# First border of a two-layer diffusion block: TensorE sums the squares tile by tile, and one low part moves ahead in the last head

## What is computed

```python
def readout(o, g):                       # HGRN2, o: heads side by side
    o = o * lax.rsqrt(jnp.mean(o * o, axis=-1, keepdims=True) + EPS)
    o = (o * norm_w.astype(jnp.float32).reshape(HG_HEADS, HG_VDIM)).reshape(b, L, D_MODEL)
    return (o * jax.nn.silu(g.astype(jnp.float32))).astype(g.dtype) @ w_out
...
x = x + mx[2] * rmsnorm(yx, post_norm[l, 0])          # and ctx likewise
hx = modulate(rmsnorm(x, pre_norm[l, 1]), mx[3], mx[4])
yx = conv_ffn(hx, ...)
```

## Time and profile before

| | us |
|---|---|
| median of 3 runs | 1404.38 |
| lowest and highest of them | 1404.37, 1404.94 |
| the profiled execution, its own time | 1403.67 |
| the profiled execution, its span | 1401.9 |
| TensorE busy in the span | 1330.2 |
| VectorE busy | 901.2 |
| ScalarE busy | 646.8 |

### The profile page before, as it was taken

The page is one execution under the profiler, slowest core; times in us unless marked ns, Lnnn a source line. Parts: engine busy times, 40 slices in busy tenths (PEclk is TensorE's granted clock), DMA queues, the critical chain, the costliest instruction groups (busy, mean ns, idle before and its releaser), DMA issues.

```text
span 1401.9 us, 21260 instructions
## 1 busy us (share of the span) xinstructions
PE 1330.2 (95%) x7893; PEld 1118.4 (80%) x7893; DVE 901.2 (64%) x1730; ACT 646.8 (46%) x1020; POOL 305.0 (22%) x203
## 2 busy tenths in 40 slices
PE   5999999999998999999999988999999988899997
PEld 3678888887765888888888756888888877899997
DVE  5567767667587744413446787777777857765573
ACT  4435444444256433223333365455555644554554
POOL 1000000000200653115541000211111300580961
PEclk9999999999999999999999999999999999999999
DMA  9543343334460632334315324433333465365743
GB/s 347 175 136 121 123 134 121 121 116 155 151 212 28 184 101 60 90 106 119 103 54 154 102 92 119 149 92 91 91 91 94 133 203 158 113 172 166 208 135 107
DMA packets 274787, 183.16 MB, mean 131 GB/s; under 512 B 6642, under 2 KB 249106, under 8 KB 274706
## 3 DMA queue, kind: packets, MB, share of 16 engines
q1 hardware_dynamic: 274162, 180.00, 42.6%
q10 hardware_dynamic: 544, 2.10, 0.4%
HBM read 181.03 MB, written 1.05 MB: 130 GB/s over the span
## 4 chain that ended last, share of the span: by engine, by line
PE 77%; DVE 13%; ACT 6%; issue 2%; DMA 1%; SPq 1%; POOL 0%; DVEq 0%; ACTq 0%
PE bank L2092 20%; PE bank L2094 20%; PE bank L2093 20%; DVE wl L1312 3%; ACT tmp L845 1%; DMA gates<-in_ada_w 1%; PE bank L2158 1%; ACT wh L799 1%; DVE hl L1408 1%; DVE tmp L1430 1%; PE bank L2207 1%; DVE conv L1760 1%; PE bank L2234 1%; PE bank L2654 1%; ACT hh L849 1%
## 5 line engine op out<-in xcount | busy, mean ns | idle before, releaser
L2092 PE MATMUL bank<-hh,wh 128*128 128x512 f32 (+1 forms) x1305 | 464.2, 356 | 11.2 <-DVE wl L1312 5.5
L2094 PE MATMUL bank<-hh,wl 128*128 128x512 f32 (+1 forms) x1305 | 459.4, 352 | 0.0
L2093 PE MATMUL bank<-hl,wh 128*128 128x512 f32 (+1 forms) x1305 | 459.1, 352 | 0.0
L799 ACT ACTIVATE wh<-wraw 128x1024 fp32r<-128x1024 f32 (+2 forms) x265 | 256.5, 985 | 100.7 <-PE bank L2094 97.4
L2092 PEld LDWEIGHTS bank<-hh,wh 128*128 128x128 f32 x1305 | 249.1, 191 | 46.4 <-DVE wl L1312 7.8
L1312 DVE TENSOR_TENSOR wl<-wraw,wh 128x1024 fp32r<-128x1024 f32 (+2 forms) x187 | 206.0, 1123 | 122.4 <-ACT wh L799 122.3
L2094 PEld LDWEIGHTS bank<-hh,wl 128*128 128x128 f32 x1305 | 248.8, 191 | 32.9
L2093 PEld LDWEIGHTS bank<-hl,wh 128*128 128x128 f32 x1305 | 249.1, 191 | 30.7
L1760 DVE SCALAR_TENSOR_TENSOR conv<-bank,pv,conv 128x189 f32<-128x189 f32 (+3 forms) x396 | 173.1, 437 | 131.8 <-ACT conv L1064 103.6
L700 POOL TENSOR_TENSOR wl<-wraw,wh 128x1024 fp32r<-128x1024 f32 x78 | 186.8, 2404 | 317.3 <-ACT wh L799 316.6
L2092 PE MATMUL bank<-fh,wh 128*128 128x512 f32 (+1 forms) x352 | 120.1, 341 | 3.4 <-DVE wl L1312 3.1
(11 more groups left out here) (331 smaller groups left out, 1905.2 us busy)
## 6 DMA issues: line engine op xcount, KB each, us to landing
wraw<-in_ffn_w_up SPq DMA_DIRECT2D x88, 512.0 KB, 3.9
araw<-in_ada_w SPq DMA_DIRECT2D x40, 1024.0 KB, 7.4
wraw<-in_mb_w_in SPq DMA_DIRECT2D x48, 512.0 KB, 4.0
wraw<-in_hg_w_in SPq DMA_DIRECT2D x40, 512.0 KB, 3.8
wraw<-in_ffn_w_down SPq DMA_DIRECT2D x32, 512.0 KB, 3.9
wraw<-in_mb_w_out SPq DMA_DIRECT2D x16, 512.0 KB, 4.7
gates<-in_ada_w SPq DMA_DIRECT2D x5, 1024.0 KB, 9.5
wraw<-in_hg_w_out SPq DMA_DIRECT2D x8, 512.0 KB, 4.7
```

The source lines that it names most:

```text
L799: act.activation(wh[:, n % SLOTS, 0:size], wraw[:, n % SLOTS, 0:size], ACT.Copy).then_inc(w_hi, 1)
L2092: pe.matmul(dst, W, hi(k), start=(k == 0), stop=False, **skip)
L2093: pe.matmul(dst, W, lo(k), start=False, stop=False, **skip)
L2094: ins = pe.matmul(dst, L, hi(k), start=False, stop=(k == nk - 1), **skip)
```

## The change

It has two parts.

At the first border DVE no longer adds the plain squares. PE multiplies each tile of squares by `ones` itself and accumulates over eight matmuls in bank 7: two of them behind y tile 4, two behind y tile 5, two behind y tile 6, and two behind y tile 7 (`square_sum`). ACT may overwrite a buffer of `sq` when PE's matmul on it (`sq_summed`) and DVE's use of it for A (`a_added`) are both done; before it waited for DVE's addition (`sq_added`). The other two borders and the final norm stay as they were, apart from the counts of `sq_added`.

In the last head `y_low(1)` moves directly behind `y_low(0)`.

```diff
         def square(m, src, n, y=False):
 
             if m >= 2:
-                user, norms = (sq_added, sqy) if y else (sq_used, sqx)
-                act.wait_ge(user, norms[0] * (KT - 2 if y else KT - 1) + m - 1)
+                if y and sqy[0] == 0:
+                    act.wait_ge(sq_summed, m - 1)
+                    act.wait_ge(a_added, m - 1)
+                else:
+                    user, norms = (sq_added, sqy) if y else (sq_used, sqx)
+                    act.wait_ge(user, (norms[0] - (1 if y else 0)) * (KT - 2 if y else KT - 1) + m - 1)
             act.activation(sq[:, m % 2, 0:n], src, ACT.Square).then_inc(sq_ready, 1)
...
@@ products (DVE)
-                dve.wait_ge(a_added, KT * i + m + 1)
-                if m > 1:
-                    dve.wait_ge(sq_added, (KT - 2) * i + m - 1)
-                V.tensor_tensor(S[:, 0:n], S[:, 0:n], sq[:, 1 - m % 2, 0:n], ALU.add).then_inc(sq_added, 1)
+                if i:
+                    dve.wait_ge(a_added, KT * i + m + 1)
+                    if m > 1:
+                        dve.wait_ge(sq_added, (KT - 2) * (i - 1) + m - 1)
+                    V.tensor_tensor(S[:, 0:n], S[:, 0:n], sq[:, 1 - m % 2, 0:n], ALU.add).then_inc(sq_added, 1)
...
@@ gate_products (DVE)
                 head_mean(HEADS - 2)
                 y_low(0)
+                y_low(1)
             dve.wait_ge(sig_ready, n + 1)
...
                 head_norm(HEADS - 2)
-                y_low(1)
             dve.wait_ge(en_ready, n + 1)
...
@@ PE
+        def square_sum(ms):
+
+            key = ("ss", 0, 0)
+            if ms[0] == 0:
+                plan.wait_free(pe, key)
+            for m in ms:
+                pe.wait_ge(sq_ready, m + 1)
+                ins = pe.matmul(bank[7][:, :], ones[:, :], sq[:, m % 2, :], start=(m == 0), stop=(m == KT - 1), skip_group_check=True)
+                if m < KT - 1:
+                    ins.then_inc(sq_summed, 1)
+            if m == KT - 1:
+                plan.done(ins, key)
+
         def both_sums(i, l, s, n):
 
             sqm[0] += KT
             even, odd = KT % 2, 1 - KT % 2
+            if i == 0:
+                square_sum(range(KT - 2, KT))
...
             if m == 4:
                 ada_turn(LATE + 2)
+            if m >= 4:
+                square_sum(range(2 * m - 8, 2 * m - 6))
```

More of the change, by code:

```diff
@@ L516, in program @@
     a_added, b_added, var_ready = sem("a_added"), sem("b_added"), sem("var_ready")
+    sq_summed = sem("sq_summed")
     x_new = sem("x_new")
@@ L751, in add_square @@
                 if m > 1:
-                    pool.wait_ge(sq_added, (KT - 2) * n + m - 1)
+                    pool.wait_ge(sq_added, (KT - 2) * (n - 1) + m - 1)
                 pool.tensor_tensor(sq[:, m % 2, 0:w], sq[:, m % 2, 0:w], sq[:, 1 - m % 2, 0:w], ALU.add).then_inc(sq_added, 1)
@@ L2385, in token_sums @@
             plan.wait_free(pe, key)
-            for j, (done, n) in enumerate(((sq_added, (KT - 2) * (sqm[0] // KT)), (sq_ready, sqm[0]))):
+            for j, (done, n) in enumerate(((sq_added, (KT - 2) * (sqm[0] // KT - 1)), (sq_ready, sqm[0]))):
                 pe.wait_ge(done, n)
@@ L2396, in both_sums @@
             even, odd = KT % 2, 1 - KT % 2
-            for key, tiles, added, most, ready in ((("ss", l, s), [sq[:, j, :] for j in range(2)], sq_added, (KT - 2) * (i + 1), sq_ready),
+            if i == 0:
+                square_sum(range(KT - 2, KT))
+            for key, tiles, added, most, ready in ((("ss", l, s), [sq[:, j, :] for j in range(2)], sq_added, (KT - 2) * i, sq_ready),
                                                    (("sb", l, s), b_sums[i], b_added, KT * i + KT - 1, b_added)):
+                if i == 0 and key[0] == "ss":
+                    continue
                 plan.wait_free(pe, key)
```

## The result

| | before | changed |
|---|---|---|
| median, same chip (us) | 1403.72 (10 runs) | 1407.65 (10 runs) |
| lowest and highest | 1402.55, 1404.94 | 1405.65, 1408.67 |
| ratio, 95% interval | | 1.0024 [1.0015, 1.0034] |
| profiled execution: own time, span | 1403.67, 1401.9 | 1408.67, 1406.9 |

The change costs 0.24%. The forecast was 1407.6. A second job with the changed kernel gave 1407.31 and 1.0015 [1.0006, 1.0025].

The account below looks back on a forecast made before the run. TensorE was taken to bound the kernel, with DVE slower at the border; 1403.67 - 0.98 + 3.24 = 1405.93 us without a clock fall, + 1.48 = 1407.41 with it, set at 1407.6, range 1405.3 to 1409.0.

Parts of the forecast that it names:

- Where the low part's gain stops: Last head: `kv` 3.2 us earlier, then `o_turn` waits 2.2 us for bank 5, leaving 0.98 us; whole gap kept: chance 0.06.
- The six products: First border: six products of `ones` by a tile ahead of y tile 7's end, 0.857 us each, 5.14 us in all.
- The rival of cheap products: Between the border's projections a product counts only one pass, 0.43 us, total 1403.4 us, or 1402.2 at 0.227; chance 0.05.
- Tile 7's copy, square and product on the path: Border's end: ACT's copy (0.57 us) and square (0.63), formerly hidden, now precede tile 7's product; L1389 starts 3.24 us later.
- the forecast with a fall: Clock falls to 1.2 GHz behind the new gap at `o_turn`, adding 1.48 us, total 1407.41; chance 0.50.
- The clock behind the moved gap: Behind the new 2.2 us wait at `o_turn` the clock may fall, costing 0 or 1.48 us; fall held a little likelier.
- Both cases: At `o_turn` the clock falls behind the new gap, chance 0.50, or does not, chance 0.31.
- No second fall at 0.5 us: Rival: clock falls at PE's 0.6 us idle before tile 7's product, 2.6 us more, 1410.0 us; chance 0.08 (or more falls).
- the case without a fall at `o_turn`: Rival: the clock does not fall behind the new gap in the last head, total 1405.9 us; chance 0.31.
- I held 0.2% to be the least: Whole kernel: no measurement tells less than 0.2%, 2.8 us, from no change; chance of within 0.2%: 0.51.
- the forecast's own step: Last head: early low part brings `o_turn` 0.98 us forward, and PE carries this without a gap to the border.

Follow-up runs that it names:

- the low part alone: Against the kernel before, only the low part of gated tile 1 moved ahead, VectorE still adding the squares: 1405.66 us (1.0007), again 1405.89 (1.0014).
- one-pass squares: The whole change, with ones and the first border's squares in the one-pass format: 1401.92 us, 0.9987 to the kernel before.
- products twice: The whole change, with each of the six inserted products issued twice: 1410.60 us, 1.0044 to the kernel before.
- sums alone: Against the kernel before, only the sums moved to TensorE, the second low part left in place: 1406.59 us, 1.0021.
- low part and mask early: Against the kernel before, low part of tile 1 and `mask_att(7, 0)` both moved ahead, VectorE still adding the squares: 1401.02 us, 0.9981.
- the kernel with GpSimd's additions: Against the kernel before, GpSimd adds the border's squares in place of VectorE, low part and `mask_att(7, 0)` early: 1406.40 us, 1.0018.

## Why the prediction was right, point by point

- *Where the low part's gain stops.* Right. The forecast had `kv` 3.2 us earlier with 0.9 us idle ahead and `o_turn` behind a wait of 2.2 us on `mask_att`, for 0.98 us; measured are 3.19 and 0.75, 2.11 and 0.90 us. Moving the mask in addition took the wait away and gave 2.19 us more, so it was the bank that held `o_turn`. That PE works without a gap from there to the border holds up to two waits of 0.4 us for DVE just ahead of and at y tile 4 (389.50 and 392.95 before), which the change left at their length.
- *The six products.* Right: 0.857 us each forecast; 0.86 in the trace, 0.86 by doubling them, and with one pass in place of them the loss turned into a gain. The rival of cheap products is excluded.
- *Tile 7's copy, square and product on the path.* Right in kind. The wait is 0.49 us against 0.6, and the variance's delay over the whole border is 3.16 us against 3.24 (from the start of y tile 4, 28.90 us before and 32.06 after). In sum, 2.26 us at the variance were forecast without a fall, 2.26 were measured in the first profile (each part was forecast 0.08 us too large, and the two errors cancel) and 3.66 in the second, where the forecast with a fall had 3.74.
- *The clock behind the moved gap.* Both cases came, one in each profile of the change, and the fall cost 1.40 us against 1.48. The chances were off as far as these few profiles tell. The wait of 2.1 us stands in six profiles (the change twice, the low part alone twice, one-pass squares, products twice), and one of them shows a fall there. The gap of 2.4 us in its old place had one in all three (before twice, sums alone). The forecast took the moved gap to be like the old one, and it was followed by a fall less often.
- *No second fall at 0.5 us.* Right in every profile of the change. So no run shows its price of 2.6 us; falls at the border cost 1.7 and 3.0 us in other kernels.
- *What I had left out.* The profiled execution took 1408.67 us, not 1405.93. The 2.26 us are in it, but it also came to the mark 0.78 us later and took 1.96 us longer behind the variance. Of these, 1.5 us were lost around the longer fall near 870 us; the other 0.5 come near 1141 us, and their cause is open. The kernel before took 1.0 us longer there in its second profile than in its first, 0.8 of it in the same place near 870 us. My sum had a fall at `o_turn` in it and nothing for falls elsewhere. So that the median of 1407.65 came so near to my 1407.6 is in part luck: the case without a fall at `o_turn` gives 1405.98 on this comparison's 1403.72, and 1.7 us of falls elsewhere would explain the rest as well. The ten executions of the change lie between 1405.65 and 1408.67, the five with a mean granted clock of 0.982 or 0.983 at 1407.96 and above, the five with 0.985 to 0.988 at 1407.34 and below. So the falls decide much of the spread, but two profiles can't say which falls.
- *What can be told apart.* I held 0.2% to be the least. The intervals here are about 0.1% to either side, and 0.13% (one-pass squares) could be told from nothing.
- *The low part alone.* By the forecast's own step it had to be 0.9 us faster. In the two comparisons it was 0.07% (which can't be told from nothing) and 0.14% slower, 1 to 2 us. The step at `o_turn` is right, but the clock fell behind the border's 2.57 us wait, and 1.7 us were lost in both profiles; of the rest, 0.6 us lie behind the variance in both. That the 0.9 us less in front of the border changed what the clock did rests on two profiles against two and is a likely cause, not a shown one; the kernel with low part and mask early waits 2.55 us at the same place, without a fall. In the change that wait no longer exists, which fits that the two parts together (2.1 and 3.4 us by the two ratios) cost less than the two alone (1 to 2 and 2.9 us).

The Trainium skill's rule ("TensorE: Matmul & The Clock Gate", Part 1: The HAM clock gate), that the monitor runs free of the kernel, agrees with the traces: the same 2.1 us gap in the same program was followed by a fall in one execution and not in the other.

## What to carry to other kernels

Before work is put on the bounding engine, read its price in its own operand format: here 0.86 us a product made a loss of what 0.23 us a product makes a gain. When a wait on the bounding engine is removed, follow that engine to its next two waits, and look who else must have moved; moving the instruction that frees the next bank brought 2.19 of the 3.09 us at `o_turn`. And of differences of 1 to 2 us in 1400, a second profile of each kernel is needed before a cause is believed, and two profiles that differ are best compared row by row along their whole length: here the same program lost 1.5 us at one fall, 450 us behind the place that was changed. A miss can hold such a fall too, as 3.0 of the 8.6 us with GpSimd did.

## What the runs showed of the hardware

- A wait of 2.1 to 2.6 us on TensorE is sometimes followed by the clock's lower level (1.2 GHz) and sometimes not: 2.4 us in its old place in three of three profiles, 2.1 us at `o_turn` in one of six, some 2.6 us at the border in two of five. The one wait of 5.55 us at the border was followed by it too. A fall cost 1.40 us in the last head, 1.7 us at the border, and 3.0 us at the border in the kernel with GpSimd's additions.
- A fall at the same place of the program can last longer in one execution than in another. The longer one cost 1.5 us more near 870 us and nothing behind the border.
- A product of a 128x128 by a 128x512 tile took TensorE 0.86 us to the next start with plain float32 operands and 0.23 us in the one-pass format, inside a dense row of others.
- GpSimd's six additions of 128x512 took 1.59 to 1.62 us four times and 2.72 and 2.75 us twice, and beside each of them one instruction or pair of VectorE took 0.9 to 1.1 us longer than before. The Trainium skill ("GPSIMD Engine Reference", 1. Specifications) says that the two engines share their memory interfaces when VectorE's instruction has two inputs there. The rows at 397.41 and 400.80 agree. At 396.27 VectorE kept its 1.21 us, and GpSimd's addition was the longer one, with 2.75 us; so one of the two was held up there as well.
